# Four PSUM banks and a longer product lag for the turned probabilities of each pair's second query block

## What is computed

```
s = einsum('bqhr,bkr->bhqk', qlb, c_kv) + einsum('bqhp,bkp->bhqk', qrb, k_r)
s = where(kpos[None, :] <= qpos[:, None], s, -inf)
p = softmax(s, axis=-1)
return einsum('bhqk,bkr->bqhr', p, c_kv)      # q in blocks of 128
```

## Time and profile before

| | before |
|---|---|
| median of 3 runs | 1296.98 us (1295.57 to 1297.92) |
| the profiled execution's own time | 1297.65 us |
| its span in the profile | 1295.9 us |
| mean granted clock of TensorE | 0.993 |
| the 16 units of the attention of the prompt | about 220 to 431 us of the span |

### The profile page before, as it was taken

How to read it: one execution, slowest core, us unless ns; L and a number is a source line. 1 busy time by engine, 2 the same in 40 slices (tenths; PEclk the granted TensorE clock), 3 DMA queues, 4 the chain that set the end, 5 groups by cost and what they waited for, 6 DMA issues and landing times.

```text
span 1295.9 us, 24153 instructions
## 1 busy us (share of the span) xinstructions
PE 1259.2 (97%) x9110; PEld 1181.9 (91%) x9110; DVE 903.9 (70%) x1470; ACT 592.9 (46%) x1222; POOL 559.1 (43%) x567
## 2 busy tenths in 40 slices
PE   9999999999999989999999999999999999999997
PEld 7888998888787559999899999999999999999987
DVE  4983167777765436188955787676776679899986
ACT  7433235665655324124454444444444544444462
POOL 0732344354431226751265977878877800000000
PEclk9999999999998999999999999999999999999998
DMA  9421102000027435630221222222222397868503
GB/s 324 144 63 34 49 5 76 5 21 1 17 70 269 156 145 201 204 119 26 84 83 60 92 74 78 90 70 92 85 75 92 122 339 262 295 196 267 164 1 139
DMA packets 70405, 151.93 MB, mean 117 GB/s; under 512 B 9138, under 2 KB 16690, under 8 KB 69842
## 3 DMA queue, kind: packets, MB, share of 16 engines
q1 hardware_dynamic: 70290, 150.39, 34.5%
HBM read 127.80 MB, written 22.56 MB: 116 GB/s over the span
## 4 chain that ended last, share of the span: by engine, by line
PE 79%; DVE 9%; issue 4%; ACT 3%; POOL 2%; DMA 2%; SPq 0%; DVEq 0%; POOLq 0%; ACTq 0%
PE ps L1196 23%; PE ps L1198 23%; PE ps L1197 23%; PE ps L1442 2%; DMA araw<-in_w_dn 1%; PE ps L1500 1%; PE ps L1454 1%; PE ps L1562 1%; PE ps L1455 1%; ACT pTH L1880 1%; DVE nmx L2735 1%; POOL chunk L1165 1%; DVE pTL L2752 1%; PE ps L1527 1%; DVE prob L2729 1%
## 5 line engine op out<-in xcount | busy, mean ns | idle before, releaser
L1165 POOL TENSOR_TENSOR chunk<-wraw,chunk 128x256 fp32r<-128x256 f32 x193 | 163.2, 869 | 100.0 <-ACT chunk L1880 99.9
L1196 PE MATMUL ps<-bHL,aHL 128*128 128x272 f32 x616 | 178.3, 289 | 2.7 <-DVE bHL L3283 2.7
L1198 PE MATMUL ps<-bHL,aHL 128*128 128x272 f32 x616 | 177.2, 288 | 0.0
L1197 PE MATMUL ps<-bHL,aHL 128*128 128x272 f32 x616 | 177.1, 288 | 0.0
L1165 POOL TENSOR_TENSOR chunk<-wsum,chunk 128x256 fp32r<-128x256 f32 x134 | 115.8, 881 | 26.7 <-ACT chunk L1880 26.5
L1880 ACT ACTIVATE chunk<-wraw 128x256 fp32r<-128x256 f32 x193 | 74.9, 412 | 104.7 <-PE ps L1198 38.4
L1196 PEld LDWEIGHTS ps<-bHL,aHL 128*128 128x128 f32 x616 | 116.0, 188 | 3.9 <-DVE bHL L3283 3.8
L1197 PEld LDWEIGHTS ps<-bHL,aHL 128*128 128x128 f32 x616 | 116.0, 188 | 0.0
L1198 PEld LDWEIGHTS ps<-bHL,aHL 128*128 128x128 f32 x616 | 115.9, 188 | 0.0
L1188 POOL TENSOR_TENSOR rt<-ms,mhalf 128x3 f32<-128x3 f32 (+1 forms) x3 | 4.4, 1463 | 246.1 <-DVE ms L3373 246.1
L1102 POOL TENSOR_TENSOR prob<-prob,rsm 128x128 f32<-128x128 f32 (+5 forms) x48 | 49.6, 1042 | 78.2 <-DVE rsm L2724 78.2
(11 more groups left out here) (494 smaller groups left out, 4605.1 us busy)
## 6 DMA issues: line engine op xcount, KB each, us to landing
araw<-in_w_dn SPq DMA_DIRECT2D x121, 256.0 KB, 3.2
wraw<-in_w_gu SPq DMA_DIRECT2D x44, 512.0 KB, 3.8
cp<-in_cache SPq DMA_DIRECT2D x64, 272.0 KB, 4.7
ab<-acts SPq DMA_DIRECT2D x34, 272.0 KB, 3.8
raw<-in_w_out SPq DMA_DIRECT2D x16, 512.0 KB, 4.3
acts<-bufC SPq DMA_DIRECT2D x22, 272.0 KB, 2.1
xt<-in_x_tok SPq DMA_DIRECT2D x9, 512.0 KB, 5.6
x<-x2s SPq DMA_DIRECT2D x8, 544.0 KB, 6.0
```

The lines of the kernel that those rows point to most:

```text
L1165: pool.tensor_tensor(x[:, 1, :], source_of(i, step), x[:, 0, :], ALU.subtract).then_inc(cw_lo, 1)
L1196: nc.tensor.matmul(out, wh, xh, start=start, stop=False, skip_group_check=onto)
L1197: nc.tensor.matmul(out, wh, xl, start=False, stop=False, skip_group_check=onto)
L1198: return nc.tensor.matmul(out, wl, xh, start=False, stop=stop, skip_group_check=onto)
```

## The change

In the wide units the transposed tiles go round the banks 4, 1, 3 and 5 in place of 4 and 5. `turn(kt)` waits for the subtraction of `kt - 4` (for `kt` below 4: for all subtractions of the unit before). `product` runs three groups behind `turn` in place of two. The wait for `vg_free` moves from `kt` 1 to `kt` 3, where bank 5 is now used first. ACT and DVE read from the new banks, in their old order. All other units stay as they were, with no instruction added or taken away.

```diff
+def wide_turn(u):
+    return u % 4 == 1
+
+def turned_bank(u, kt):
+    return (4, 1, 3, 5)[kt % 4] if wide_turn(u) else 4 + (tr_count(u) + kt) % 2
+
+def turned_before(u, kt):
+    x = tr_count(u) + kt
+    if not wide_turn(u):
+        return x - 1
+    return x - 3 if kt >= 4 else tr_count(u)
+
+def product_lag(u):
+    return 3 if wide_turn(u) else 2
...
                     if x >= 2:
-                        pe.wait_ge(t_free, x - 1)
+                        pe.wait_ge(t_free, turned_before(u, kt))
...
-                        last = nc.tensor.transpose(ps[:, 4 + x % 2, P * qi:P * qi + P], prob[:, at:at + P],
+                        last = nc.tensor.transpose(ps[:, turned_bank(u, kt), P * qi:P * qi + P], prob[:, at:at + P],
...
-                for kt in range(nk + 2):
+                lag = product_lag(u)
+                for kt in range(nk + lag):
...
-                    elif u % 4 == 1 and kt == 1:
+                    elif u % 4 == 1 and kt == 3:
                         pe.wait_ge(vg_free, 2 * (u // 4) + 2)
                     if kt < nk:
                         turn(kt)
-                    if kt >= 2:
-                        product(kt - 2)
+                    if kt >= lag:
+                        product(kt - lag)
...
-                    hi(pTH[:, x % 4, c0:512], ps[:, 4 + x % 2, c0:512]).then_inc(t_hi, 1)
+                    hi(pTH[:, x % 4, c0:512], ps[:, turned_bank(u, kt), c0:512]).then_inc(t_hi, 1)
...
-                    nc.vector.tensor_tensor(pTL[:, x % 4, c0:512], ps[:, 4 + x % 2, c0:512],
+                    nc.vector.tensor_tensor(pTL[:, x % 4, c0:512], ps[:, turned_bank(u, kt), c0:512],
```

## The result

Over 22 runs each the changed kernel has a median of 1299.6 us (1295.64 to 1305.15) and the kernel before 1297.31 us (1295.27 to 1300.18): a ratio of 1.0018, 95% interval 1.0010 to 1.0026. The change costs about 0.2%, and its runs scatter twice as far. That is still inside the 0.2% within which the prediction calls a kernel the same, but the interval lies wholly above 1, so the loss is real. The forecast was 1296.3 us with a range of 1294.0 to 1298.6; the time lies above it. The profiled execution is the slowest of the 22, 1305.15 us, and so shows the loss larger than it mostly is.

A forecast was written before the change was run, and what follows sets the result against it. It took a cycle of ACT and DVE waiting for each other to bound the wide units, with PE's waits its lateness. Four units at 0.16 us gave 1296.98 - 0.64 = 1296.3 us, range 1294.0 to 1298.6.

The forecast's parts named there:

- list of gaps on ACT and DVE: In wide units, gaps of 0.66, 0.76, 0.47, 0.57 and 0.32 us would stay the same, with the same releasers.
- step (a): Wait for vg_free moved to kt 3: earlier turn(1) lets ACT's copy of group 1 start sooner, 0.16 us per wide unit.
- (b): Four banks: the 0.25 and 0.22 us waits ahead of turn(6) and turn(7) go, but nothing is gained.
- (c): Product lag of three: PE finishes transpositions early, then waits for the same three subtractions; nothing gained by itself.
- (d): turn(0) waits for all subtractions of the unit before, in place of all but one; costs nothing.
- rival 1: Faster: twice the banks let ACT and DVE close their gaps too; in full 1290.5 us; chance 0.11.
- The sum: Wide units shrink from 10.83 to 10.67 us; four save 0.64 us in all.
- Rival 2: Slower: TensorE's clock falls in a wide unit's last 3 us; 1300.8 us once, 1314 in all four; chance 0.06.
- The price: Cost of a clock fall: 10 us at half clock lose 4.5 us; in all four wide units 18 us.

The follow-up runs named there:

- e5: The kernel before, with DVE's addition of the weighed values moved in the wide units behind the subtraction of group 3; 1294.37 us, ratio 0.9986.
- e2: The changed kernel with only the wait for the values moved: wide units on banks 4 and 1, lag two; 1296.33 us, ratio 0.9993.
- e3: The changed kernel, four banks and moved wait, but products two groups behind instead of three; 1299.4 us, ratio 1.0018.
- e8: The changed kernel with lag two and each turn(kt) held back until the subtraction of kt - 2; 1295.71 us, ratio 0.9991.
- e4: The changed kernel with the two banks and waits of the kernel before, products still three groups behind; 1297.53 us, ratio 1.0002.
- e9: The changed kernel with 1, 1 and 3 extra matmuls of ones ahead of product(4), product(5) and product(6) of each wide unit; 1296.04 us, ratio 0.9994.
- e11: The kernel before, with the pTH matmul left out of product(4) and product(5) in wide units; 1300.88 us, ratio 1.0026.
- e7: The kernel before with the wait for the values moved (banks 4 and 1, lag two) and DVE's addition later, as in e5; 1294.71 us, ratio 0.9979.

## Why the prediction was wrong

**Where the time lies: right.** It said that 1.63 us of PE's idle time in a wide unit are the lateness of a cycle between ACT and DVE, and that the wait would go from the transpositions to the products. The waits are 1.47 us ahead of three products, as forecast. Its list of gaps on ACT and DVE was less good: 0.57 and 0.32 us stayed, but 0.66 and 0.76 us grew by 0.21 each, and 0.47 us shrank to 0.30, as step (a) implied; the list did not carry that through. And e5 showed the cycle directly: moving 0.67 us of DVE's work shortened the unit by 0.57 us.

**Step (a), 0.16 us: right in size and in cause.** The unit is 0.16 us shorter up to `product(6)`, and e2, which makes this step alone, has it too (0.15 us a pair).

**Steps (b), (c) and (d), nothing: right at full clock.** e3 and e8 have the period of e2, and e4 has that of the kernel before, within 0.03 us. That answers rival 1 too: twice the banks closed no gap between ACT and DVE by themselves.

**The sum: right for an execution without falls, and not what was measured.** Four times 0.16 us, 0.64 us, is what e2 and e9 show within their error (both medians 1.1 us below that of the kernel before run beside them, 1297.47 and 1297.18, with intervals of 0.1% to either side).

**The failed step: the fall of the clock was put at nothing in the sum.** Rival 2 named its place and its mechanism, and both are what happened. I gave it 0.06, and the range did not reach it. The argument against it was a single stretch from 7 to 10 us in which PE was busy 1.52 of 3 us at a clock of 1.00, and "at least 1.53 us of work" after the change. The amount was right, 1.54 of 3 us at the end of the first wide unit, and behind it the clock was 0.50 all the same. A clock that did not fall in one place of one execution was taken as a sign that it would not fall. But whether it falls differs from run to run: the changed kernel's runs have mean clocks from 0.987 to 0.994, and e3's profiled execution had no fall at the wide units where half of its runs were low. The comparison that would have told something was like with like: the end of the wide unit held 1.88 us of work before and about 0.35 us of that, the last transpositions, were about to be moved out of it. I had the figure and read it the wrong way.

**The price, too, was mis-sized.** I took 10 us at half clock and 4.5 us from the sample stage, 18 us for four. A fall behind a wide unit mostly lasts a third as long and costs 1.3 to 1.6 us (2.8 us the one that lasted twice as long); all four cost 7.4 us, and that in the slowest execution. On the mean of the runs the change lost 1299.84 - 1296.06 = 3.8 us against e9, which has the same products and waits and no run of low clock. At 1.5 us each that would be two or three falls a run, an estimate which takes the sample stages to be alike. So the result lies between the forecast and the 1300.8 us that one fall of the rival would have given. That it still counts as the same, to which I gave 0.82, is luck: there are several falls, each at a third of my price. Also, "fell once" was not exact for the kernel before: the clock was at 0.50 too in its last 5.9 us (from 1290.00), where PE does nothing.

**The page and the runs.** The Trainium skill, TensorE: Matmul & The Clock Gate, "A second HAM failure mode: psum-queue depth-cycling", tells of PSUM cycling and short idle times between groups together. Of the two, the runs bear out the idle times and not the cycling: e8 cycles through four banks at a mean clock of 0.994, and e11 falls with two. The Trainium skill, TensorE: Matmul & The Clock Gate, "Part 4: PE-mode transpose", says that transposing does not count as busy in the same way. The runs speak against that for this kernel: e3 and e8 differ only in when the transpositions run, and their low runs are 6 of 12 and 0 of 11. Whether a transposition counts as much as a product, no run here shows.

**What stays open.** Why a given execution falls and the next one does not, and how much work is enough, was not tried. Nor was any such move in the units with `u % 4 == 3`. The low runs of e5 and e7 (3 and 2 of 11), with 2.20 and 2.24 us of work in the last 3 us, are not explained.

## What to carry to other kernels

When PE waits for a cycle between two other engines, letting it run ahead gained nothing here, and it emptied the very stretch in which it then waited. Only once that cycle was shorter did four banks give something, 0.12 us a pair. Before giving an engine more buffers, list who releases each gap of the engines that it waits for; if they release each other, move work in their lists first. And when idle time of TensorE is brought together, even by tenths of a microsecond, compare the mean granted clock of many runs, not the clock row of one profile.

## What the runs showed of the hardware

Less work made the kernel slower: without eight matmuls it took 1300.88 us where the kernel before took 1297.17, and five matmuls a unit that compute nothing brought 1299.6 down to 1296.04. The difference is PE's clock: it fell to half (granted clock 0.50) behind the wide units from whose end work had been taken, in some executions of a program and not in others, for 1.3 to 1.6 us a fall of some 3 us.
